# A two-block network on one core: first expert's rows by a product, results in the weights' queue, and other edits

## The reference

```python
for l in range(2):                                  # first block
    sh1, sc1, gt1, sh2, sc2, gt2 = split(silu(c) @ w_ada[l] + b_ada[l], 6)
    xn = modulate(rms_norm(h, g_norm_mix[l]), sh1, sc1)
    p = xn @ w_in[l]                                # U, V, VA, KA, QA, KC, VC, QC, gates
    y_a = diff_post(diff_attention(qa, ka, va, lam), da_subln_g[l])
    y_b = spatial_gating(p[..., U and V])
    y_c = neighbourhood_attention(qc, kc, vc, rpb)
    h = h + gt1 * (merge_branches(y_a, y_b, y_c) @ w_out[l])
    xn2 = modulate(rms_norm(h, g_norm_ffn[l]), sh2, sc2)
    h = h + gt2 * hier_moe(xn2, ...)                # 32 experts, two for each token
h = rms_norm(h, g_final)
# second block: gated linear attention, short convolution and dilated attention of h,
# merged by gates, then a gated feed-forward with a causal convolution

def hier_moe(x):                                    # t tokens
    group = argmax(x @ w_group + b_group)
    two experts of the group by top_k, weights by softmax
    sort the 2 t (token, choice) pairs by expert, in padded blocks of rows
    y = (silu(xs @ w_gate[e]) * (xs @ w_up[e])) @ w_down[e]
    add each row, times its weight, to its token
```

## Time and profile before

| | us |
|---|---|
| median of 3 runs | 2766.84 (2762.44 to 2771.36) |
| the profiled execution | 2769.21 |
| its span, first to last instruction | 2767.3 |

### The profile page before, as it was taken

How to read it: one execution, slowest core, us unless ns; L and a number is a source line. 1 busy time by engine, 2 the same in 40 slices (tenths; PEclk the granted TensorE clock), 3 DMA queues, 4 the chain that set the end, 5 groups by cost and what they waited for, 6 DMA issues and landing times.

```text
span 2767.3 us, 30439 instructions
## 1 busy us (share of the span) xinstructions
PE 2519.1 (91%) x12204; PEld 1526.6 (55%) x12204; DVE 764.0 (28%) x1607; ACT 470.1 (17%) x1056; POOL 175.3 (6%) x202
## 2 busy tenths in 40 slices
PE   8999999999987778799999999777779999998998
PEld 4444544445544444445577655443445788885873
DVE  1784444215311111154243230000002323212220
ACT  2121223101110100022122111000001212202320
POOL 0000000000111111100000011111110000000000
PEclk9999999999999999999999999999999989999999
DMA  7454010424999999954424599999994423343441
GB/s 297 182 213 182 31 62 31 175 99 182 371 426 426 426 426 425 401 216 199 166 92 156 218 376 424 425 425 426 425 380 186 152 92 122 115 153 148 152 151 57
DMA packets 60218, 664.83 MB, mean 240 GB/s; under 512 B 12885, under 2 KB 13173, under 8 KB 21073
## 3 DMA queue, kind: packets, MB, share of 16 engines
q1 hardware_dynamic: 45072, 630.48, 56.1%
q0 software_dynamic: 14176, 29.73, 2.9%
q10 hardware_dynamic: 864, 3.15, 0.3%
HBM read 663.24 MB, written 21.02 MB: 247 GB/s over the span
## 4 chain that ended last, share of the span: by engine, by line
PE 70%; DMA 24%; DVE 2%; issue 1%; ACT 1%; POOL 0%; SPq 0%; DVEq 0%; ACTq 0%; POOLq 0%
DMA ring<-in_w_moe 12%; PE act_bank L687 7%; PE act_bank L676 6%; PE act_bank L796 6%; DMA xT<-in_w_moe 5%; PE act_bank L1170 5%; PE vec_bank L812 4%; PE vec_bank L968 4%; PE score_bank L796 4%; PE score_bank L1057 4%; PE vec_bank L1067 3%; PE vec_bank L796 3%; PE act_bank L1402 3%; PE vec_bank L1402 3%; PE vec_bank L1420 3%; DMA values<-in_w_moe 3%
## 5 line engine op out<-in xcount | busy, mean ns | idle before, releaser
L676 PE MATMUL act_bank<-ring,xT 128*128 128x512 f32 x448 | 195.7, 593 | 1.6 <-ACT xT L1536 1.5
L687 PE MATMUL act_bank<-xT,ring 128*128 128x512 f32 (+1 forms) x512 | 193.6, 539 | 0.0
L2390 DVE TENSOR_TENSOR heads<-work,vec_bank 128x256 f32<-128x256 f32 x64 | 26.9, 421 | 526.5 <-PE vec_bank L1057 526.3
L796 PE MATMUL act_bank<-xT,ring 128*128 128x256 f32 (+1 forms) x576 | 157.8, 427 | 1.9 <-issue 1.5
L687 PEld LDWEIGHTS act_bank<-xT,ring 128*128 128x128 f32 x512 | 97.1, 190 | 95.4 <-issue 92.2
L1057 PE MATMUL vec_bank<-ring,branches 128*64 128x256 f32 x1024 | 118.8, 385 | 28.7 <-DMA ring<-in_w_moe 28.7
L1057 PE MATMUL score_bank<-ring,branches 128*64 128x256 f32 x1024 | 120.4, 388 | 25.6 <-issue 12.9
L1067 PE MATMUL vec_bank<-ring,heads 128*64 128x512 f32 x512 | 116.9, 598 | 28.4 <-DMA ring<-in_w_moe 20.4
L676 PEld LDWEIGHTS act_bank<-ring,xT 128*128 128x128 f32 x448 | 83.9, 190 | 104.5 <-issue 101.8
L796 PEld LDWEIGHTS act_bank<-xT,ring 128*128 128x128 f32 x576 | 109.2, 190 | 44.1 <-issue 32.0
L1170 PE MATMUL act_bank<-xT,ring 128*128 128x256 f32 x576 | 128.6, 386 | 0.6 <-ACT work L1802 0.6
(11 more groups left out here) (405 smaller groups left out, 3381.7 us busy)
## 6 DMA issues: line engine op xcount, KB each, us to landing
ring<-in_w_moe SPq DMA_DIRECT2D x96, 2048.0 KB, 36.8
ring<-in_w_in SPq DMA_DIRECT2D x31, 2048.0 KB, 8.5
ring<-in_w_merge SPq DMA_DIRECT2D x27, 2048.0 KB, 7.7
ring<-in_w_ada SPq DMA_DIRECT2D x24, 2048.0 KB, 9.5
branches<-in_w_moe SPq DMA_DIRECT2D x24, 2048.0 KB, 36.9
heads<-in_w_moe SPq DMA_DIRECT2D x24, 2048.0 KB, 36.9
xT<-in_w_moe SPq DMA_DIRECT2D x24, 2048.0 KB, 36.8
values<-in_w_moe SPq DMA_DIRECT2D x24, 2048.0 KB, 37.0
```

The lines of the kernel that those rows point to most:

```text
L676: mm = pe.matmul(b.t[:, :], xT[:, k, tile * P:(tile + 1) * P], w[:, k * COLS:(k + 1) * COLS], start=(k == 0), stop=(k == KD - 1))
L687: mm = pe.matmul(b.t[:, 0:n], w[:, k * COLS + f * P:k * COLS + (f + 1) * P], xT[:, k, 0:n], start=(k == 0), stop=(k == KD - 1))
L796: mm = pe.matmul(g.t[:, 0:n], merge_tile(l, i, MERGE_TILES * d + k), xs[:, k, 0:n], start=(k == 0), stop=(k == KD - 1))
```

## The change

Five edits.

1. **Route and first expert.** The block of a pair comes from one broadcast comparison and one sum. The first expert's rows (expert 0) are taken by a product: VectorE writes for each tile a matrix of 64 columns that marks its tokens, PE multiplies the normed tiles with it (`first_rows`, eight products of 64x512 in layer 0, four in layer 1) ahead of the hot products, ScalarE copies them, and PE turns them between the first and the second half of the hot products. The gather of expert 0 is gone and with it `turn_tokens(0)` and ten fillers. SP's load into `values`, which waited for that gather, waits for the product.
2. **Results.** SP's queue reads them: y0, U, y1, V, y2, VA, y3 (in the second block y0, v, y1, dv0). They wait for the last expert's gate product, not its up product. POOL's small loads ahead of the next layer, or ahead of the second block, wait for y1's landing.
3. **Boundaries on PE.** `last_sum` of tile 1 stands between the fillers (6 and 6, or 8 and 10), before the first product and no longer in it, and PE waits for the first weights behind the sums.
4. **Fillers** ahead of the last tile in differential attention (10), in `merge_out` (10), and ahead of `norm2_columns` (20).
5. **Modulation.** The first norm and part 2's turn stand ahead of the last part; fillers behind go from 8 to 4.

The core of the diff:

```diff
@@ -631,18 +636,19 @@
             pe.wait_ge(cond_zero.sem, 1)
             parts = []
             for j in range(ADA_FIRST):
+                if j == ADA_FIRST - 1:
+                    norm_tile(l, 0)
+                    turn_ada_part(j - 1, parts[j - 1])
                 ada_part(l, j, A[j % 2])
                 parts.append(let_go(A[j % 2]))
                 if j == 0:
                     spread_rows()
-                else:
+                elif j < ADA_FIRST - 1:
                     turn_ada_part(j - 1, parts[j - 1])
-                if j == ADA_FIRST - 2:
-                    norm_tile(l, 0)
             b = V[0]
             turn_ada_part(ADA_FIRST - 1, parts[-1]).then_inc(b.full, b.fill())
             mark["mod", l] = let_go(b)
-            keep_going(8)
...
-
             def gate_tile(tile):
                 b = V[tile % 2]
                 pe.wait_ge(vv_done.sem, vv_done.take("pe"))
@@ -730,20 +734,20 @@
 
             def next_tile(tile):
                 norm_tile(l, tile)
-                if l >= 1 and 1 <= tile and tile + 1 < NT:
+                if l >= 1 and 1 <= tile < NT - 1:
                     last_sum(l - 1, tile + 1)
 
             if l >= 1:
                 last_sum(l - 1, 0)
-                keep_going(12)
+                keep_going(6)
+                last_sum(l - 1, 1)
+                keep_going(6)
             if l >= 1:
                 next_tile(0)
+            wu = slot_of(("in", l, "U"))
             for tile in range(nt):
                 normed(l, tile)
-                rows_group(A[0], wu, tile, 0, KD // 2)
-                if l >= 1 and tile == 0:
-                    last_sum(l - 1, 1)
-                rows_group(A[0], wu, tile, KD // 2, KD)
+                rows_group(A[0], wu, tile)
                 mark["u", l, tile] = let_go(A[0])
                 if tile == 0:
...
@@ -883,6 +887,9 @@
             attend(items, scores, weigh, value, 1,
                    lambda i: merge_between(l, 0, i, len(items) // MERGE_UNITS, V[2], V[3]))
             for tile in range(tiles(l)):
+                if tile == tiles(l) - 1:
+                    pe.wait_ge(S[0].free, S[0].fills)
+                    keep_going(10, S[0])
                 pe.wait_ge(o_done.sem, o_done.take("pe"))
                 turn_rows(o_rows, tile)
...
             turn_normed(nt - 1)
             logits(l, nt - 1)
 
-        def keep_going(n):
+        def keep_going(n, b=V[3]):
 
...
@@ -1034,13 +1043,32 @@
                 .then_inc(b.full, b.fill())
...
             for q in range(2 * nt):
+                if q == nt:
+                    turn_first_rows()
                 pe.wait_ge(hot_done.sem, hot_done.take("pe"))
                 mm = pe.matmul(b.t[:, 0:N_BLK * N_EXP], hot_slot[:, q, :], hot_place[:, q, :], start=(q == 0), stop=(q == 2 * nt - 1))
             mm.then_inc(b.full, b.fill())
-            keep_going(10)
+
+        def first_rows(l):
+
+            b = A[0]
+            pe.wait_ge(first_hot.sem, l + 1)
+            pe.wait_ge(b.free, b.fills)
+            for g in range(2):
+                for tile in range(tiles(l)):
+                    mm = pe.matmul(b.t[g * CAP:(g + 1) * CAP, :], hot_first[:, tile, :], xn2[:, tile, g * HALF:(g + 1) * HALF],
+                                   start=(tile == 0), stop=(tile == tiles(l) - 1))
+            mm.then_inc(b.full, b.fill())
+            mark["first_rows", l] = at_bank(b)
+
+        def turn_first_rows():
+            pe.wait_ge(A[0].free, A[0].fills)
+            pe.wait_ge(A[1].free, A[1].fills)
+            turn_half_rows(xg[:, 0, :], A[1], 4).then_inc(A[1].full, A[1].fill())
...
             wv = slot_of(("in2", 2, "v"))
-            rows2_tile(wv, 0, A[0], 0, KD // 2)
-            last_sum(DEPTH - 1, 1)
-            rows2_tile(wv, 0, A[0], KD // 2, KD)
+            rows2_tile(wv, 0, A[0])
             wd = slot_of(("in2", 2, "dv0"))
             rows2_tile(wd, 0, A[1], 0, KD // 2)
...
@@ -1461,6 +1487,8 @@
         for tile in range(2):
             for c in range(OUT_CHUNKS):
                 out_product(2, tile, c, 0, KD)
+        pe.wait_ge(V[0].free, V[0].fills)
+        keep_going(20, V[0])
         norm2_columns()
         feed_forward()
...
@@ -2329,12 +2358,21 @@
                 step(nc.vector.tensor_reduce(r["pos"][:, :, k:k + 1], r["w1"], X, ALU.add))
             nc.vector.tensor_copy(r["cnt"], b.t[:, NT * N_EXP:(NT + 1) * N_EXP]).then_inc(b.free, b.read())
             pos, blk = r["pos"], r["blk"]
-            step(TS(blk, pos, float(CAP), None, ALU.is_ge))
-            for n in range(2, N_BLK):
-                step(STT(out=blk, in0=pos, scalar=float(n * CAP), in1=blk, op0=ALU.is_ge, op1=ALU.add))
+            flat = "p t k -> p (t k)"
+            wide = [P, 2 * nt, N_BLK - 1]
+            reached = r["w2"].rearrange(flat)[:, 0:2 * nt * (N_BLK - 1)].rearrange("p (q n) -> p q n", n=N_BLK - 1)
+            step(STT(out=reached, in0=pos.rearrange(flat).unsqueeze(2).to_broadcast(wide), scalar=1.0 / CAP,
+                     in1=C("iota")[:, 1:N_BLK].unsqueeze(1).to_broadcast(wide), op0=ALU.mult, op1=ALU.is_ge))
+            step(nc.vector.tensor_reduce(blk.rearrange(flat), reached, X, ALU.add))
             step(STT(out=pos, in0=blk, scalar=float(-CAP), in1=pos, op0=ALU.mult, op1=ALU.add))
             for k, idx in ((0, r["i1"]), (1, r["i2"])):
                 step(STT(out=blk[:, :, k:k + 1], in0=blk[:, :, k:k + 1], scalar=float(N_EXP), in1=idx, op0=ALU.mult, op1=ALU.add))
+            key, first = r["w1"][:, :, 0:2], r["w1"][:, :, 2:3]
+            wide = [P, nt, CAP]
+            step(STT(out=key, in0=blk, scalar=float(CAP), in1=pos, op0=ALU.mult, op1=ALU.add))
+            step(nc.vector.tensor_reduce(first, key, X, ALU.min))
+            TT(hot_first[:, 0:nt, :], C("places")[:, 0:CAP].unsqueeze(1).to_broadcast(wide), first.to_broadcast(wide),
+               ALU.is_equal).then_inc(first_hot.sem, first_hot.up())
...
@@ -2821,6 +2859,8 @@
             if l == 0:
                 pool.dma_start(sgw[:, :, :], t["sg_w"][l]).then_inc(rows_in[l], 16)
                 return
+            pool.wait_ge(*mark["last_read", l - 1])
+            pool.wait_ge(y_in[1], 16 * l)
             modulation_columns()
             pool.dma_start(cond_rows[:, 0:streams(l), :], t["cond_rows"][0:streams(l), :].unsqueeze(0)
...
@@ -2863,7 +2903,6 @@
                 .then_inc(scattered[b], 16)
 
         def experts(l):
-            gather(l, 0)
             gather(l, 1)
...
@@ -2941,9 +2969,9 @@
                 power(rstd[:, tile:tile + 1], rstd[:, tile:tile + 1])
             dispatch(l)
             experts(l)
-            results(l)
 
         pool.wait_ge(*mark["moe_end", DEPTH - 1])
+        pool.wait_ge(y_in[1], 16 * DEPTH)
         pool.dma_start(dil_mask.rearrange("p d t n -> p (d t n)"), t["dil_masks"]).then_inc(block2_in[0], 16)
         pool.dma_start(pos_i, t["positions"].to_broadcast([P, SEQ])).then_inc(block2_in[0], 16)
...
@@ -3031,7 +3059,7 @@
                 sp.wait_ge(*mark["logits", l])
             elif home == 3:
                 sp.wait_ge(x_stored[l], 16 * tiles(l))
-                sp.wait_ge(gathered[0], 16 * (N_EXP // 2 * l + 1))
+                sp.wait_ge(*mark["first_rows", l])
             sp.dma_start(ring[NSLOT + home][:, 0:SLOT], source(c)).then_inc(ring_loaded[NSLOT + home], 16)
...
@@ -3064,16 +3092,29 @@
             for c in range(3 * (N_EXP - MOE_AHEAD), 3 * N_EXP):
                 load(("expert", l, c))
 
-        def results_first(l):
-
-            sp.wait_ge(y_in[0], 16 * l)
+        def result(l, tile):
+
+            y2 = y_rows[l].rearrange("(t k) n -> t (k n)", k=2)
+            if tile == 0:
+                for b in range(2):
+                    sp.wait_ge(scattered[b], 16 * (N_EXP // 2 - b) * (l + 1))
+                sp.wait_ge(zeroed, 16 * (l + 1))
+                sp.wait_ge(*mark["last_gate", l])
+            if tile == NT - 1:
+                sp.wait_ge(*mark["last_read", l])
+            sp.dma_start(y_tile[tile], y2[tile * P:(tile + 1) * P, :]).then_inc(y_in[tile], 16)
+
+        result_ahead = {("in", 1, "U"): (0, 0), ("in", 1, "V"): (0, 1), ("in", 1, "VA"): (0, 2),
+                        ("in2", 2, IN2_ORDER[0]): (1, 0), ("in2", 2, IN2_ORDER[1]): (1, 1)}
 
         for l in range(DEPTH):
             for c in ORDER:
                 if c[1] == l and c[0] != "expert" and BEFORE[c] is not None:
-                    if l >= 1 and c == ("in", l, "V"):
-                        results_first(l)
+                    if c in result_ahead:
+                        result(*result_ahead[c])
                     load(c)
+                    if c == ("in", 1, "VA"):
+                        result(0, NT - 1)
                     if c == ("in", 0, "V"):
                         load_rows(2)
```

39 lines of the change are left out of this document (18 added, 21 removed).

## The result

| | before | changed |
|---|---|---|
| median, us (7 runs each) | 2764.2 (2761.96 to 2771.36) | 2759.59 (2757.09 to 2761.22) |
| span of the profiled execution | 2767.3 | 2757.3 |
| PE busy | 2519.1 (91%) | 2525.3 (92%) |
| VectorE busy | 764.0 | 763.7 |
| POOL busy | 175.3 | 169.5 |

The medians lie 4.6 us apart (0.17%). The ratio on record, over all the runs, is 0.9974 (0.26% less), with a 95% interval of 0.9962 to 0.9986, so the kernel is faster, by very little. 2761.7 was predicted. The two profiled executions differ by 10.0 us of span, about twice the medians' difference, so the traces are read place by place.

What follows compares the result with a forecast made beforehand. TensorE was taken to hold 70% of the end and transfers, the expert stages, 24%. Terms 2.7 - 6.0 + 2.8 - 2.9 - 0.7 - 2.4 + 1.8 - 0.4 = -5.1 us took 2766.84 to 2761.7, range 2748 to 2772.

Steps and rivals of the forecast that it cites:

- the 47%: Whole kernel: the chance, 0.47, given to a result within 0.3% of the time before.
- differential, layer 0: Ten fillers before differential attention's last tile: 2.2 us late, 1.8 back on scores, 1.1 on turns and rotations: -0.7.
- norm2's columns: Twenty fillers ahead of norm2's columns: 3.1 us late, 1.3 given back on the records behind: +1.8.
- POOL's wait: Boundary to layer 1: POOL's power queued behind the wait for y1 and five issues, at 1181.2, not 1179.49: +1.7 us.
- D's interleaving: Slower rival, 2775: y1 shares the engines with loads behind it, landing up to 13 us later; chance 0.14.
- The first expert in layer 0: Layer 0's route: hot products end at 697.4, 4.1 us late; gated product moves +3.9, to 711.75.
- The down product behind it issues nothing sooner either: Layer 0: the first down product follows the gated product's +3.9 us; SP's load at 713.02 waits on its end.
- the bound becomes VectorE: Layer 1: up complete by 1610, VectorE's queue done at 1612.85, so the gated product comes 5.35 us sooner.
- of the 3.9 us 2.7 reach the stream: Layer 0's weights stream: the fourth load's data could have flowed about 1.2 us sooner before, so the delay costs +2.7.
- The product's length: First rows' product: 6.0 us for layer 0's eight, between 3.65 and 7.3; 2.6 us for layer 1's four.
- Rival B: Faster rival, 2752.5: the first rows' product overlaps, at 3.65 us, and the clock holds; chance 0.30.
- C, the gain of layer 1 is not kept: Rival, 2767: layer 1's sooner start is not kept and its -6.0 us shrinks to nothing; chance 0.14.

Runs made afterwards that it cites:

- Experiment 5: The changed kernel without POOL's two waits for the landing of y1: 2745.8 us, ratio 0.9934 against the kernel before.
- experiment 1: The changed kernel with the first rows' product ordered tile by tile, both column halves in turn: 2756.5 us, ratio 0.9974 against the kernel before.
- experiments 2 and 3: Changed kernel; 2 moves VectorE's list ahead of its wait for hot products: 2760.0 us; 3 also moves turn of expert 1's rows behind down product: 2757.8 us.
- experiment 4: Changed kernel with list, turn and halves reordered, no y1 wait, fewer fillers: 2740.0 us; last run also issues expert 2's gather earlier, 13 norm2 fillers: 2734.3 us.

## Why the prediction was right, and where it was not

Its total was right: 2761.7 against 2759.59, and nearly "no difference", as the 47% had it. Some of that is luck: the steps below missed by up to 1.9 us each, both ways, and the spans of the two traces differ by twice what the medians do. Step by step, from the traces (after less before; the rest of the kernel also differs, by about -3 in all, which is part of why these spans differ by more than the medians):

| step | predicted | measured |
|---|---|---|
| start | -0.4 | -0.05 |
| differential, layer 0 | -0.7 | +0.4 |
| merge's tile, route, first expert, layer 0 | +2.7 | +1.75 |
| boundary to layer 1 | +2.8 | +3.45 |
| differential, layer 1 | -2.4 | -2.65 |
| merge's tile, route, first expert, layer 1 | -6.0 | -7.0 |
| boundary to the second block | -2.9 | -2.8 |
| norm2's columns | +1.8 | -0.1 |
| sum | -5.1 | -7.0 |

**POOL's wait** was the step on which the forecast hung, and it was right in mechanism, and nearly in size: power at 1183.22, 2.0 later than forecast, while the stage had ended 2.55 later. y1 landed 11.23 us after its issue, 12.1 after y0's, near the 12.4 that 4 MB in order had been taken for, so D's interleaving did not come. By the Trainium skill, "DMA: Bandwidth & Descriptors", Queues, rings and completion order, one row's ring goes in order; the trace agrees: at the boundary to the second block the three landed at 2070.39, 2075.29 and 2077.77, in the order of issue. The clock fell, though the fillers ended 2.9 us ahead of the transposes and not 4 and more, and it cost somewhat more than I had taken: 2.8 us on the first products (2.2 in the sum), and some 1.1 on the transposes and copies ahead of them, which no term had. Experiment 5 shows both halves of the price.

**The first expert in layer 0** was right up to the gated product: 711.74 against 711.75. That is closer than the working deserves: its terms add up to 698.0 and not to the 697.4 written there, the product began 0.5 later than taken and took 5.42 and not 6.0, and the hot products and transposes behind it took 4.1 and not 4.7. Behind it two steps failed. "The down product behind it issues nothing sooner either" took that product at its old 3.65; after 7.31 idle microseconds it began at the low clock, 4.99, and in layer 1 6.37, where "the bound becomes VectorE" stopped one step too soon. And "of the 3.9 us 2.7 reach the stream" was a slack of 1.2; in truth the load came 5.9 us later (A) and the stage ended 3.0 later (B), so nearly 3 were absorbed. The three loads that went out sooner are the likely reason, and that a gather and the reads at the end are gone; no run parts these.

**The product's length** was placed rightly between its ends in layer 0; in layer 1 the same price, 2.6 us for four, was too high: 1.94, for the reason that experiment 1 gives. Rival B had layer 0's at 3.65; experiment 1 shows that this is the price of another order. The Trainium skill, "TensorEngine Tiling (Array Packing)", Key Properties, has different tiles work in parallel; both traces agree, 3.65 for different tiles in turn, and 5.42 where the second tile's records began only with the fifth of the first's.

**Fillers.** Norm2's +1.8 was mis-sized: the turns were late by 2.7 (3.1 had been taken), but the clock gave back 1.6 on the records behind (I had taken 1.3) and 1.1 on turns and copies, which I had not counted. Differential attention in layer 0 went the other way: 1.9 late, near the 2.2 computed, and the scores stayed at the low clock (4.54, as before), so the 1.8 taken for them did not come in this trace. In those of experiments 2 and 3 it did, with the same code. What decides there is open.

**What I did not see** is that the change leaves some 25 us of median. Of these the traces give 11.9 to the wait, 4.7 to list, turn and order in layer 0 (B 488.69 in the last run of experiment 4), and 0.9 to layer 1. The rival "C, the gain of layer 1 is not kept" did not happen in the change; in experiments 3 and 4 a further start of layer 1 was not kept, by a path that none of my rivals had.

## What to carry to other kernels

When transfers move to another queue, look at what *waits* for them in the old one: here two waits for a landing, placed ahead of small loads that nobody needed yet, held the one engine that raises to a power, and cost the part all of the 9 us that it is worth. A stage that is bound by its stream is worth its start only while the transfers still have gaps: look at GB/s by windows first. Where they have, the start is a chain across four engines, and shortening one link shows the next one (list, gather's turn, gather's landing), so move the chain link by link and read the trace each time. A filler belongs in a pause only as long as the pause is; but what it buys behind itself, in products at the high clock, can be more than what it costs (2.65 us gained in layer 1's differential attention). Before one trace is taken to say what fillers did to the clock, look at the same place in other runs of the same code.

## What the runs showed that I had not expected

A gather of one expert's rows (128x512, 0.25 MB) took 3.30 us with idle engines, 7.88 us with two or three weights' loads under way, 9.8 with a full weights' queue, and 20.25 to 21.48 us behind four small loads in POOL's list as well, though at the stream's 425 GB/s its bytes are 0.6 us. Eight products of 64x512 took 3.65 us or 5.42, by nothing but their order, and four took 1.94 in both orders. And the same code at 271 us (L796, now L800, twelve records) took 7.33 us before and 7.77 in the changed kernel, with no edit near it.
